# x's tiles 2 and 3 loaded when tiles 0 and 1 have landed, the first weight tile ahead of them in two halves, x's first and last tile transposed and split in halves

## What is computed

```python
z = x @ w_in[l]
h_a, b_a, c_a, x_r, y_r, g_a, g_r = jnp.split(z, SPLITS, axis=-1)
...
xc = causal_dwconv(x_r, conv_r_w[l]) + conv_r_b[l]
r_gate = jax.nn.sigmoid(block_diag(xc, w_rg_a[l], b_rg_a[l]))
i_gate = jax.nn.sigmoid(block_diag(xc, w_rg_x[l], b_rg_x[l]))
log_a = -RG_C * r_gate.astype(jnp.float32) * jax.nn.softplus(-rg_lambda[l].astype(jnp.float32))
```

## Time and profile before

| what | value |
|---|---|
| median of 3 runs | 833.96 us (833.56 to 834.3) |
| profiled execution, span from the first to the last instruction | 831.3 us |
| PE busy | 821.0 us (99%) |
| DVE, ACT, POOL busy | 579.2, 450.6, 73.3 us |
| share of PE in the chain that ended last | 97% |

### The profile page before, as it was taken

One profiled execution on the slowest core, in us unless ns is written; L12 is line 12 of the kernel. 1 busy time (PEld: TensorE's weight loads), 2 busy tenths in 40 slices (PEclk: granted clock), 3 DMA queues, 4 the chain that ended last, 5 costly groups with the idle time before them and its releaser, 6 DMA issues.

```text
span 831.3 us, 11149 instructions
## 1 busy us (share of the span) xinstructions
PE 821.0 (99%) x3833; PEld 682.0 (82%) x3833; DVE 579.2 (70%) x672; ACT 450.6 (54%) x456; POOL 73.3 (9%) x73
## 2 busy tenths in 40 slices
PE   9999999999999999999999999999999999999995
PEld 8888888888888888888888888888888888888873
DVE  5877434434557885432455588898899899899978
ACT  4655424433466663333233333578887887878640
POOL 1000000100000000000000000622211111100121
PEclk9999999999999999999999999999999999999999
DMA  6333324553233323234432926699999999999582
GB/s 209 93 109 90 101 84 148 200 177 101 76 101 101 101 88 114 85 94 139 151 90 77 352 102 253 203 320 418 388 393 397 395 394 390 400 377 384 227 317 106
DMA packets 112338, 173.45 MB, mean 209 GB/s; under 512 B 7402, under 2 KB 90003, under 8 KB 100534
## 3 DMA queue, kind: packets, MB, share of 16 engines
q1 hardware_dynamic: 106486, 159.80, 54.7%
q0 software_dynamic: 5824, 13.30, 4.4%
HBM read 163.49 MB, written 16.30 MB: 216 GB/s over the span
## 4 chain that ended last, share of the span: by engine, by line
PE 97%; DVE 2%; ACT 0%; issue 0%; DVEq 0%; POOL 0%; POOLq 0%
PE psA L689 8%; PE psA L691 8%; PE psA L690 8%; PE psA L876 7%; PE psA L878 7%; PE psA L877 7%; PE psB L691 6%; PE psB L690 6%; PE psB L689 6%; PE psB L903 3%; PE psB L902 3%; PE psB L901 3%; PE psD L691 2%; PE psC L691 2%; PE psD L690 2%; PE psC L689 2%
## 5 line engine op out<-in xcount | busy, mean ns | idle before, releaser
L1588 DVE TENSOR_TENSOR elo<-est,ehi 128x2048 fp32r<-128x2048 f32 x94 | 211.1, 2287 | 26.0 <-ACT ehi L1206 25.8
L1206 ACT ACTIVATE ehi<-est 128x2048 fp32r<-128x2048 f32 x94 | 177.6, 1917 | 41.5 <-DMA est<-in_w_exp_down_dram 24.9
L1378 DVE TENSOR_TENSOR wlo<-wst,whi 128x1024 fp32r<-128x1024 f32 (+1 forms) x76 | 95.0, 1251 | 86.5 <-ACT whi L1037 85.3
L1037 ACT ACTIVATE whi<-wst 128x1024 fp32r<-128x1024 f32 (+1 forms) x76 | 81.9, 1078 | 77.2 <-PE psB L691 30.7
L876 PE MATMUL psA<-ehi,xe_hi 128*128 128x512 f32 x256 | 101.4, 396 | 0.0
L878 PE MATMUL psA<-ehi,xe_lo 128*128 128x512 f32 x256 | 100.0, 390 | 0.0
L877 PE MATMUL psA<-elo,xe_hi 128*128 128x512 f32 x256 | 99.7, 390 | 0.0
L689 PE MATMUL psB<-xT_hi,whi 128*128 128x512 f32 x208 | 81.1, 390 | 0.0
L691 PE MATMUL psB<-xT_hi,wlo 128*128 128x512 f32 x208 | 81.0, 389 | 0.0
L690 PE MATMUL psB<-xT_lo,whi 128*128 128x512 f32 x208 | 81.0, 389 | 0.0
L878 PEld LDWEIGHTS psA<-ehi,xe_lo 128*128 128x128 f32 x256 | 48.1, 188 | 10.2
(11 more groups left out here) (371 smaller groups left out, 1536.3 us busy)
## 6 DMA issues: line engine op xcount, KB each, us to landing
est<-in_w_exp_gate_dram SPq DMA_DIRECT2D x32, 1024.0 KB, 12.3
est<-in_w_exp_up_dram SPq DMA_DIRECT2D x32, 1024.0 KB, 11.4
est<-in_w_exp_down_dram SPq DMA_DIRECT2D x32, 1024.0 KB, 12.5
wst<-in_w_in_dram SPq DMA_DIRECT2D x60, 512.0 KB, 3.9
wst<-in_w_branch_r_dram SPq DMA_DIRECT2D x8, 640.0 KB, 4.3
ys<-zero POOLq DMA_DIRECT2D x8, 512.0 KB, 2.9
wst<-in_w_branch_a_dram SPq DMA_DIRECT2D x8, 512.0 KB, 3.6
o_st<-in_w_out_dram SPq DMA_DIRECT2D x8, 512.0 KB, 4.4
```

What stands on the lines that cost most here:

```text
L1037: A(whi[p][:, 0:K, :], wst[p][:, 0:K, :], ACT.Copy).then_inc(w_hi, 1)
L1206: A(ehi[s][:], est[s][:], ACT.Copy).then_inc(gu_hi if s < 4 else d_hi, 1)
L1378: V.tensor_tensor(wlo[p][:, 0:K, :], wst[p][:, 0:K, :], whi[p][:, 0:K, :], ALU.subtract).then_inc(w_lo, 1)
L1588: V.tensor_tensor(elo[s][:], est[s][:], ehi[s][:], ALU.subtract).then_inc(gu_lo if s < 4 else d_lo, 1)
```

## The change

SP issues weight tile 0 as two halves of k (0 to 3, 4 to 7), each with its own semaphore. It waits until x's tile 0 has landed before it issues tile 2, and until tile 1 has landed before tile 3. The order of issue stays. ACT and DVE make `whi` and `wlo` of that weight tile in two halves. x's tiles 0 and 3 signal after four transposes and after eight, and ACT and DVE split them in halves. On PE the filler of 17 matmuls becomes 7, two more are put between tiles 2 and 3, all of `first_half` moves behind the transposes of tile 3, and the transpose of `rows` moves from ahead of the second column half to behind it. On DVE `wlo` of tile 1 comes ahead of the copy of `chan`.

```diff
             load_x(0)
             load_x(1)
-            load(0, 0, part(win_v, COL_XR, 0))
+            sp.dma_start(wst[0][:, 0:KD // 2, :], part(win_v, COL_XR, 0)[:, 0:KD // 2, :]).then_inc(first_landed, 16)
+            sp.dma_start(wst[0][:, KD // 2:KD, :], part(win_v, COL_XR, 0)[:, KD // 2:KD, :]).then_inc(w_landed[0], 16)
+            sp.wait_ge(x_landed[0], 16)
             load_x(2)
+            sp.wait_ge(x_landed[1], 16)
             load_x(3)
...
                 for k in range(KD):
                     mm = pe.transpose(psC[t % 2][:, k // 4, (k % 4) * P:(k % 4 + 1) * P],
                                       x1[:, t, k * P:(k + 1) * P], ident[:])
+                    if k == 3 and t in X_SPLIT:
+                        mm.then_inc(xt_t, 1)
                 mm.then_inc(xt_t, 1)
...
             x_back(1)
-            early_warm(17)
+            early_warm(7)
             x_back(2)
+            early_warm(2)
+            x_back(3)
+            pe.wait_ge(first_lo, 1)
+            pe.wait_ge(xt_lo, x_parts(2))
+            first_half(range(KD // 2))
             pe.wait_ge(w_lo, 1)
-            pe.wait_ge(xt_lo, 2)
-            first_half(range(2))
-            x_back(3)
-            first_half(range(2, KD))
-            pe.wait_ge(rows_landed, 16 * 8)
-            pe.transpose(psB[0][:, 0:NROW], rows[0:NROW, :], ident[0:NROW, 0:NROW]).then_inc(chan_t, 1)
+            first_half(range(KD // 2, KD))
...
-            pe.wait_ge(xt_lo, TT)
+            pe.wait_ge(xt_lo, x_parts(TT))
             product(psA[0][:, SH:S], (whi[0], wlo[0]), [buf[:, :, SH:S] for buf in (xT_hi, xT_lo)], KD
                     ).then_inc(tile_done, 1)
+            pe.wait_ge(rows_landed, 16 * 8)
+            pe.transpose(psB[0][:, 0:NROW], rows[0:NROW, :], ident[0:NROW, 0:NROW]).then_inc(chan_t, 1)
             xr(1, 1, first=True)
...
                 if t == 1:
-                    lo(0, 0)
+                    dve.wait_ge(first_hi, 1)
+                    V.tensor_tensor(wlo[0][:, 0:KD // 2, :], wst[0][:, 0:KD // 2, :], whi[0][:, 0:KD // 2, :],
+                                    ALU.subtract).then_inc(first_lo, 1)
+                    dve.wait_ge(w_hi, 1)
+                    V.tensor_tensor(wlo[0][:, KD // 2:KD, :], wst[0][:, KD // 2:KD, :], whi[0][:, KD // 2:KD, :],
+                                    ALU.subtract).then_inc(w_lo, 1)
+            lo(1, 1)
             dve.wait_ge(chan_t, 1)
             V.tensor_copy(chan[:, 0:NROW], psB[0][:, 0:NROW]).then_inc(chan_ready, 1)
-            lo(1, 1)
```

More of the change, by code:

```diff
@@ L243, in trunk_moe @@
         w_landed = [sem(f"w_landed{p}") for p in range(3)]
+        first_landed = sem("first_landed")
+        first_hi = sem("first_hi")
+        first_lo = sem("first_lo")
         w_hi = sem("w_hi")
@@ L360, in trunk_moe, with x_parts, x_cut @@
         NROW = C_BN + KD
+        X_SPLIT = (0, TT - 1)
+        def x_parts(t):
+            return t + sum(u < t for u in X_SPLIT)
+        def x_cut(t, q):
+            ks = slice(4 * q, 4 * q + 4) if t in X_SPLIT else slice(0, KD)
+            banks = slice(q, q + 1) if t in X_SPLIT else slice(0, 2)
+            return (psC[t % 2][:, banks, :].rearrange("p a (b c) -> p (a b) c", c=P),
+                    xT_hi[:, ks, t * P:(t + 1) * P], xT_lo[:, ks, t * P:(t + 1) * P])
         block = ctx.enter_context(nc.Block())
@@ L647, in x_back @@
                 if t >= 2:
-                    pe.wait_ge(xt_lo, t - 1)
+                    pe.wait_ge(xt_lo, x_parts(t - 1))
                 for k in range(KD):
@@ L1039, in _ @@
             for t in range(TT):
-                act.wait_ge(xt_t, t + 1)
-                A(xT_hi[:, :, t * P:(t + 1) * P], psC[t % 2][:].rearrange("p a (b c) -> p (a b) c", c=P),
-                  ACT.Copy).then_inc(xt_hi, 1)
+                for q in range(1 + (t in X_SPLIT)):
+                    act.wait_ge(xt_t, x_parts(t) + q + 1)
+                    turned, x_hi, _ = x_cut(t, q)
+                    A(x_hi, turned, ACT.Copy).then_inc(xt_hi, 1)
                 if t == 1:
-                    hi((0, 0), 0, first=True)
+                    act.wait_ge(first_landed, 16)
+                    A(whi[0][:, 0:KD // 2, :], wst[0][:, 0:KD // 2, :], ACT.Copy).then_inc(first_hi, 1)
+                    act.wait_ge(w_landed[0], 16)
+                    A(whi[0][:, KD // 2:KD, :], wst[0][:, KD // 2:KD, :], ACT.Copy).then_inc(w_hi, 1)
             hi((1, 0), 1, first=True)
@@ L1381, in _ @@
             for t in range(TT):
[L1382 to L1385, removed]
+                for q in range(1 + (t in X_SPLIT)):
+                    dve.wait_ge(xt_hi, x_parts(t) + q + 1)
+                    turned, x_hi, x_lo = x_cut(t, q)
+                    V.tensor_tensor(x_lo, turned, x_hi, ALU.subtract).then_inc(xt_lo, 1)
                 if t == 1:
-                    lo(0, 0)
+                    dve.wait_ge(first_hi, 1)
[5 more added lines that the diff above has]
+            lo(1, 1)
             dve.wait_ge(chan_t, 1)
             V.tensor_copy(chan[:, 0:NROW], psB[0][:, 0:NROW]).then_inc(chan_ready, 1)
-            lo(1, 1)
             e, s1, s2, acc = (decay[:, n, :] for n in (2, 3, 4, 5))
```

## The result

The changed kernel takes 836.53 us (median of 5 runs, 835.03 to 837.77), the kernel before 833.56 us on the same chip (5 runs, 833.12 to 834.3). The ratio is 1.0035 [1.0023, 1.0046]: slower by 3.0 us, by more than the 0.2% that can be told here. The forecast was +2.15 us and slower, the range 834.4 to 838.4 holds the time, and the wait that was to appear before `rg(0)` is there. One of the signs that the prediction had named as showing it wrong is there too, a stretch at half clock in the first 30 us, so the sum is made of other parts than forecast, as the next views show.

What follows compares the result with a forecast made beforehand. TensorE was taken to bound the kernel, with DVE some 0.1 us behind at `rg(0)`. Tile 3's transposes starting at 11.3, less 9.15, gave +2.15 us on 833.96: 836.1 us, range 834.4 to 838.4.

Steps and rivals of the forecast that it cites:

- a stretch at half clock in the first 30 us: Sign named as showing the prediction wrong: TensorE granted half its clock near the start of the kernel.
- The row it turned on: DVE's timeline before `rg(0)`: `xc_lo` ends at 24.11, leaving DVE some 0.1 us behind being the bound.
- PE's own work: PE from tile 3's transposes on: `rows` transpose 6.65 us after their start, `xr(1)` ending 12.3 us after it.
- B: Start of x's tile 3's transposes on PE, taken as 11.3 us, between a landing at 10.3 and one at 11.9.
- The `chan` chain: DVE and ScalarE from the copy of `chan` to `xc_lo`, 8.12 us; PE then waits about 2.8 us at `rg(0)`.
- No second wait at `rg(1)`: DVE's next steps shift with `chan` and stay some 0.5 us ahead of `rg(1)`; no second wait charged.
- case (c): Rival at the start's loads: x's tile 3 lands early, at 9.7 to 10.8; +0.5 to +1.7 us; chance 0.25.
- B - 9.15: Shift of `rg(0)`, and so of the kernel's end, from before: 11.3 - 9.15 = +2.15 us.
- Case (d): Rival: PE's clock falls in the new wait before `rg(0)`, losing 1.7 us, giving 837.8 us; chance some 0.1.
- The constant: Difference between the profiled span, 831.3, and the median of the runs, 833.96: 2.66 us, taken as unchanged.
- The loads held back: SP issues x's tiles 2 and 3 later, at about 4.5 and 5.7 us; forecast as covered, delaying no landing.
- the 10.3 end: Early landing of x's tile 3, at 10.3 us, if nothing of w_in's tile 1 runs ahead of it.

## Why the prediction was right, point by point

- **The row it turned on.** "DVE is here only some 0.1 us behind being the bound": right. Moving one 120-column transpose on PE made DVE's chain the bound, and putting it back removed both the wait and the loss (832.67). Of the signs named, `rg(0)` was to come at about 26.4 and came at 25.98; DVE's idle time behind `chan` was to be 0.7 and was 0.83.
- **PE's own work.** `rows` at B + 6.65: measured B + 6.69. End of `xr(1)` at B + 12.3: B + 12.42 (the chain's idle piece starts at 23.16).
- **The `chan` chain.** `chan` at B + 6.96: B + 6.99. ScalarE's part uncovered, `decay` 1.78 after `chan`: 1.79, with 0.83 of idle time of DVE. `xc_lo` ended 8.12 after `chan`: 8.14. `rg(0)` at B + 15.14: B + 15.24, and B + 15.16 to B + 15.23 in three more profiles of this order. The wait, 2.8 us: 2.82.
- **No second wait at `rg(1)`.** Right for the change. The run with `decay` moved shows how near it was: 2.00 us taken from one wait gave 1.61 in the other.
- **B was mis-sized.** The term taken was 11.3; after shows 10.74, case (c)'s range rather than the forecast's. Its 0.56 us go straight into the sum: B - 9.15 is 1.59, not 2.15. The step that failed is taking the load's own landing of before, 11.9, as the upper end and leaning towards it. That is one execution's number: the same issues in the run with only the transpose moved gave 7.5 us to landing where the earlier trace rows have 9.0. In the nine profiles in which tile 3's transposes follow tile 2's and two fillers, B was 10.68 to 11.50, so the value taken is inside the spread but no better than any other in it.
- **The clock was under-weighed.** Case (d) had 0.1 and "neither is as long as that stretch" against it. That argument does not hold: it sets the length of an idle time against that of the half-clock stretch in the earlier trace rows, ahead of which PE had not been idle at all. The fall came in three of three profiles of the changed order on PE and DVE as it stood, for 3.4 us, and cost 1.6 to 1.7 us. Cases (c) and (d) came together, 1.69 + 1.69 = 3.4 us in the trace, where I had priced them as alternatives: (c) alone says no change that can be told, (d) alone 837.8. The miss of B hid the miss of the clock: that 836.1 lies so near the result is luck.
- **The constant.** The sum took 2.66 us between span and time. The changed kernel's profiled execution took 836.53 us with a span of 834.9: 1.6 apart, and 1.6 to 1.9 in every other. So the profiled execution of before stood 0.6 to 0.8 us under its median (831.3 + 1.65 against 833.56 here and 833.75 over 24 runs), which is why the spans differ by 3.6 and the medians by 2.97.
- **The loads held back.** Worth nothing that can be seen: without SP's waits the tile is used at the same time and the kernel takes as long (836.55 and 836.53). The prediction covered the later issue, rightly, but still let the hold-back pull B down by the 10.3 end ("if nothing of tile 1 runs ahead"); what brought B from 12.43 to about 11 was that PE had less to do ahead of tile 3, no six products and eight filler matmuls fewer. The profiles of the old order show it: with all the filler B was 12.43, 13.13 and 13.31, although in the second of them tile 3 had landed at 10.4.

## What to carry to other kernels

Before a small operation is moved on the engine that bounds the kernel, follow its result through the other engines to where the bounding engine needs it, and measure the slack there: here a transpose of 120 columns, moved behind 2.9 us of other matmuls, cost 3.9 us, some 1.6 of them by the clock, since the slack was 0.1. When a change opens a new idle stretch on TensorE, sum it twice, with and without a stretch at half clock behind it, and add that to the other cases instead of setting it against them. A start that hangs on a landing, read from one profile, is a draw from a spread, here 0.8 us wide (10.68 to 11.50), and so is a span against its median.

## What the runs showed of the hardware that was not expected

- A wait of 2.8 us of TensorE was followed by a stretch of some 3.4 us at a granted clock of 0.50 in three of three profiles of the changed kernel's PE order (waits ending at 25.98, 26.06 and 25.84), but not in the profile of the kernel before with the transpose moved (2.80, ending at 28.07), nor behind a wait of 1.79. In all three the clock was still at 1.00 during the wait; it fell 0.1, 0.9 and 1.4 us after PE had begun to work again. With filler in the wait it did not come (0.57 us idle left). What decides between 2.82 and 2.80 us is open; no run told it apart.
- The half-clock stretch near 506 us, in narrow matmuls without an idle stretch, comes in some executions (before, and four others) and is absent in the rest, with no difference in the time behind `rg(0)`.
- The same load issued at the same time in the same order took 9.0 us in one execution and 7.5 us in another from issue to landing.
- At the start TensorE runs at half its later pace although the profile grants 1.00 there: 14 filler records in 3.36 us, 0.24 each, in 1.10 to 4.50 us of the profile before, and 0.112 each from 6.78 on. When the pace rises differs from execution to execution: tile 0's eight transposes took 1.12 us in one profile of the old order and 1.94 in the three others.
